# The low parts of the expert weights: from VectorE and GpSimd to VectorE alone, one operation per half chunk

## The reference

```python
def moe(x, w_router, b_router, w_gate_up, b_gate_up, w_down, b_down):
    logits = (x @ w_router) + b_router
    top_v, top_e = lax.top_k(logits, TOP_K)          # 4 of 32 experts for each row
    gates = jax.nn.softmax(top_v, axis=-1)
    ...
    def expert_block(args):
        xb, e = args
        h = xb @ w_gate_up[e] + b_gate_up[e]         # 1024 -> 2048
        gate = jnp.minimum(h[:, 0::2], SWIGLU_LIMIT)
        up = jnp.clip(h[:, 1::2], -SWIGLU_LIMIT, SWIGLU_LIMIT)
        glu = gate * jax.nn.sigmoid(gate * SWIGLU_ALPHA)
        return ((up + 1.0) * glu) @ w_down[e] + b_down[e]
    ...
    return jnp.sum(picked * gates[..., None], axis=1)
```

## Time and profile before

| | |
|---|---|
| times of three runs | 1637.43, 1633.67, 1636.84 us; median 1636.84 us |
| the profiled execution, from its first to its last instruction | 1633.7 us (no time of its own is given beside this span) |
| TensorE busy | 1552.0 us (95%) |
| VectorE busy | 1343.2 us (82%) |
| ScalarE busy | 937.3 us (57%) |
| GpSimd busy | 648.7 us (40%) |
| mean granted TensorE clock | 0.965 of full speed |

### The profile page before, as it was taken

The page is one execution under the profiler, slowest core; times in us unless marked ns, Lnnn a source line. Parts: engine busy times, 40 slices in busy tenths (PEclk is TensorE's granted clock), DMA queues, the critical chain, the costliest instruction groups (busy, mean ns, idle before and its releaser), DMA issues.

```text
span 1633.7 us, 19999 instructions
## 1 busy us (share of the span) xinstructions
PE 1552.0 (95%) x7028; PEld 1092.7 (67%) x7028; DVE 1343.2 (82%) x1571; ACT 937.3 (57%) x863; POOL 648.7 (40%) x229
## 2 busy tenths in 40 slices
PE   6999799959999999999999999999999999999992
PEld 4877585437676777776777777677777677767762
DVE  3034304469999999999999999999999999999995
ACT  2023411137666666666666666666666666666663
POOL 1011300024554444544445544555445544444443
PEclk9999859969999999999999999999999999999996
DMA  9300307138999999999999999999999999999974
GB/s 353 138 5 0 130 23 298 55 128 324 343 342 349 336 340 343 349 340 348 344 346 345 334 338 344 339 337 348 341 330 346 345 346 334 348 337 344 342 292 135
DMA packets 52241, 468.06 MB, mean 287 GB/s; under 512 B 9370, under 2 KB 13420, under 8 KB 27156
## 3 DMA queue, kind: packets, MB, share of 16 engines
q1 hardware_dynamic: 40676, 441.39, 71.2%
q0 software_dynamic: 9488, 22.99, 6.9%
q10 hardware_dynamic: 2032, 3.12, 0.6%
HBM read 451.15 MB, written 22.46 MB: 290 GB/s over the span
## 4 chain that ended last, share of the span: by engine, by line
PE 79%; DVE 4%; DMA 1%; issue 1%; ACT 0%; POOL 0%; DVEq 0%; ACTq 0%; POOLq 0%
PE psum L1497 23%; PE psum L1499 21%; PE psum L1498 21%; PE psum L1444 4%; PE psum L1511 3%; DVE low L1130 2%; PE psum L1467 2%; PE psum L1486 1%; PE psum L1477 1%; PE psum L1524 1%; PE psum L1427 0%; DMA y_tbl<-area,idx_i 0%; DVE ring L1187 0%; PE psum L1420 0%; ACT high L682 0%
## 5 line engine op out<-in xcount | busy, mean ns | idle before, releaser
L1130 DVE TENSOR_TENSOR low<-raw,high 128x1024 fp32r<-128x1024 f32 x645 | 953.3, 1532 | 24.9 <-ACT high L682 24.9
L682 ACT CAST high<-raw 128x2048 fp32r<-128x2048 f32 x387 | 732.6, 1909 | 179.7 <-PE psum L1499 168.5
L457 POOL TENSOR_TENSOR low<-raw,high 128x1024 fp32r<-128x1024 f32 x129 | 468.7, 3633 | 643.3 <-ACT high L682 630.1
L1497 PE MATMUL psum<-high,area_r 128*104 128x512 f32 x1536 | 621.9, 405 | 0.8 <-DVE area_r L1123 0.3
L1499 PE MATMUL psum<-low,area_r 128*104 128x512 f32 x1536 | 604.3, 393 | 0.0
L1498 PE MATMUL psum<-high,area_r 128*104 128x512 f32 x1536 | 604.1, 393 | 0.0
L1497 PEld LDWEIGHTS psum<-high,area_r 128*104 128x104 f32 x1536 | 257.9, 168 | 132.9 <-issue 45.9
L1499 PEld LDWEIGHTS psum<-low,area_r 128*104 128x104 f32 x1536 | 258.1, 168 | 96.3
L1498 PEld LDWEIGHTS psum<-high,area_r 128*104 128x104 f32 x1536 | 258.8, 168 | 83.4
L696 ACT ACTIVATE area<-area 104x512 f32<-104x512 f32 x64 | 40.5, 633 | 166.4 <-DVE area L1138 166.4
L1233 PE MATMUL psum<-ring 128*128 128x272 f32 x416 | 96.6, 393 | 0.0
(11 more groups left out here) (199 smaller groups left out, 1020.6 us busy)
## 6 DMA issues: line engine op xcount, KB each, us to landing
raw<-in_w_gate_up SPq DMA_DIRECT2D x130, 2048.0 KB, 10.3
raw<-in_w_down SPq DMA_DIRECT2D x64, 2048.0 KB, 8.2
ring<-in_w_in SPq DMA_DIRECT2D x1, 4096.0 KB, 37.0
area<-in_w_out SPq DMA_DIRECT2D x1, 4096.0 KB, 34.4
ring<-in_w_in SPq DMA_DIRECT2D x1, 3072.0 KB, 22.8
area<-in_x_prompt SPq DMA_DIRECT2D x4, 512.0 KB, 8.3
ring<-in_w_mem_kv SPq DMA_DIRECT2D x1, 2048.0 KB, 14.6
ring<-in_mem_kT SPq DMA_DIRECT2D x1, 2048.0 KB, 9.3
```

Source lines behind the costliest of these rows:

```text
L457: nc.gpsimd.tensor_tensor(low_w(t, 1, 2), raw_w(t, 1, 2), high_w(t, 1, 2), ALU.subtract).then_inc(sem("w_low_pool"), 1)
L682: nc.scalar.copy(high_w(t), raw_w(t)).then_inc(sem("w_high"), 1)
L1130: last = v.tensor_tensor(low_w(t, part, 2), raw_w(t, part, 2), high_w(t, part, 2), ALU.subtract)
L1497: mm(bank, high, wh, start=False, stop=False)
```

## The change

All twelve low parts of an expert come from VectorE, each in one operation of 2048 columns. GpSimd's `low_part` goes, and with it the semaphore `w_low_pool` and TensorE's wait on it.

```diff
-POOL_T = (2, 5, 8, 11)
...
-            def low_part(n, t):
-
-                pool.wait_ge(sem("w_high"), n * HALVES + (t + 1))
-                nc.gpsimd.tensor_tensor(low_w(t, 1, 2), raw_w(t, 1, 2), high_w(t, 1, 2), ALU.subtract).then_inc(sem("w_low_pool"), 1)
...
             def expert(n, k):
                 if not isinstance(n, int) or n > 0:
                     scatter(n, k)
-                low_part(n, 5)
                 gather(n + 1, k + 1)
-                low_part(n, 8)
-                low_part(n, 11)
-                low_part(n + 1, 2)
 
             gather(0, 0)
-            low_part(0, 2)
...
             def low_part(n, t):
 
-                parts = 1 if t in POOL_T else 2
                 dv.wait_ge(sem("w_high"), n * HALVES + (t + 1))
-                for part in range(parts):
-                    last = v.tensor_tensor(low_w(t, part, 2), raw_w(t, part, 2), high_w(t, part, 2), ALU.subtract)
-                last.then_inc(sem("w_low"), 1)
+                v.tensor_tensor(low_w(t), raw_w(t), high_w(t), ALU.subtract).then_inc(sem("w_low"), 1)
...
             def split_done(n, t):
 
                 pe.wait_ge(sem("w_low"), n * HALVES + (t + 1))
-                if t in POOL_T:
-                    pe.wait_ge(sem("w_low_pool"), n * len(POOL_T) + (POOL_T.index(t) + 1))
```

## The result

The changed kernel takes 1646.39 us (median of 4 runs, 1643.84 to 1648.30), against 1636.91 us before (4 runs): 9.5 us more, ratio 1.0065, 95% interval 1.005 to 1.008. The profiled execution spans 1646.5 us; its time was 1648.30, so 1.8 us lie outside the span.

A forecast was written before the change was run, and what follows sets the result against it. TensorE was taken to bound the kernel; 10.6 us of new wait less 1.3, 1.2 and 0.3 gave +7.8 us, profiled execution 1641.5 and median 1644.6. Range 1641 to 1650, or 1633 to 1650 with no new wait.

The forecast's parts named there:

- TensorE sets the pace: In the expert loop TensorE's matmuls bound the time, 38.855 us an expert; relieving VectorE by itself is worth nothing.
- The load itself: VectorE's work for each expert in the loop: 37.7 us before, 33.4 after, under TensorE's 38.855.
- The price of the long operation: A VectorE low part of 2048 columns lasts 2.285 us and takes 2.20 us of the queue.
- The freed memory: With GpSimd's part gone, VectorE's low parts run undisturbed: all within 2.26 to 2.35 us, none of 3 us or more.
- The new wait: TensorE waits for the second `act_low` ahead of half chunk 10: 0.33 us for each expert, 10.6 us in all.
- the handover from `act_low` to TensorE: Ahead of half chunk 10, TensorE's matmul starts 0.06 us after `act_low` ends, taken from one earlier case.
- The start gives back 1.3 us: Start of the loop: three VectorE operations take 6.60 us ahead of `x_low` where five took 7.92, so 1.3 us gained.
- The end gives back 1.2 us: End of the loop: without GpSimd's unneeded low part, the last scatter starts 0.19 us behind `yrow`, 1.2 us earlier.
- The median: Whole kernel: the profiled 1633.7 us was put 3.1 under the median of 1636.84; the median would go to 1644.6.
- The rivals: No new wait, 0.25; low parts keep their mean, 0.02; the freed engine is worth something, 0.05; a larger wait, 0.05.
- The case of no new wait: Rival: `act_low` is in time ahead of half chunk 10, leaving only the 2.8 us given back: 1634.0 us; chance 0.25.
- a slightly quicker TensorE: Rival: TensorE gains 0.1 us an expert with no new wait, 1630.8 us; 0.05 together with VectorE setting the pace.

The follow-up runs named there:

- twelve_ahead: The changed kernel with the low part of the next expert's half chunk 0 also ahead of the second `act_low`: 1744.2 us, 1.067 of the kernel before.
- only_eleven_pool: The changed kernel with the second 1024 columns of half chunk 11 given back to GpSimd: 1627.4 us, 0.994 of the kernel before.
- act_low_first: The changed kernel with the second `act_low` moved between the low parts of half chunks 10 and 11: 1627.1 us, 0.994 of the kernel before.
- eleven_to_dve: The kernel before with half chunk 11 alone taken from GpSimd, made by VectorE in two operations of 1024 columns: 1700.6 us, 1.038.

## Why the prediction was right, point by point

- **TensorE sets the pace, and VectorE's load doesn't.** Right: VectorE's busy share went from 194 to 180 us in 200, and the time rose. `twelve_ahead` shows it most plainly. The load itself was put too low, 33.4 us for each expert; measured are 179.77 / 200 x 39.29 = 35.3. The rest beside the low parts was taken as 7.0 from durations that count every overlap twice (20 x 1.535 = 30.7); the busy time in the earlier trace rows, 853.0 / 576 x 20 = 29.6, leaves 8.1. And the twelve long operations are busy for 871.8 / 387 x 12 = 27.0 us, not 26.4. With 4 us of slack left this cost nothing.
- **The price of the long operation: 2.285 us, of which 2.20 lie in the queue.** Measured 2285 ns in the median, and 821.74 to 826.15 for two, 2.205 each. The Trainium skill's formula (page "VectorE: DVE Perf Modes", section on the TRN2 errata) gives 2.29 us; the trace agrees within 0.01.
- **The freed memory.** Right: no operation over 2.295 us. In none of the six kernels without a low part on GpSimd does one of 2048 columns take over 2.30 us, or one of 1024 over 1.23. The trace agrees with the Trainium skill's rule that an operation of VectorE with two inputs and one of GpSimd that reads the memory lock each other out (page "SBUF — State Buffer", section "Who interferes with whom"): 3443 ns at most before, 2295 after. `only_eleven_pool` shows the other side: GpSimd's part takes 5.15 to 5.17 us each time, and none of VectorE's low parts is held up.
- **The new wait, 0.33 us for each expert, 10.6 us.** The place, the engines and the chain are right: swiglu at 0.43 us (measured 0.42), 2.73 us to the low parts (2.73), 4.40 for these (4.41). The size was 0.43 us and 13.8 us. The term that was mis-sized is the handover from `act_low` to TensorE: "the matmul started at 433.19, 0.06 later", where it is 0.13 us in the median of every kernel that waits there. That row lies in expert 1, ahead of the loop, where the handover is 0.06 us in each kernel; 28 of the 32 experts lie inside it. With it the same expert gives 0.40 us, as measured in the two shown (8.27 against 7.87); over all experts the old stretch is 7.83. And one step was misread: "Before, it started at 821.61, right behind the transposes". It started 0.13 us behind the end of `act_low`, 820.90 + 0.58 = 821.48, so it waited already. This wait of 0.21 us in each expert had no entry of its own, since the eight transposes are shown as lasting until 821.58. It cancels out of the difference of the two kernels: the change made a wait of 0.65 us out of one of 0.21. But it made the room for gain larger than I thought.
- **The start gives back 1.3 us.** Measured 1.2.
- **The end gives back 1.2 us.** Measured 1.2, but not in the way foretold: the scatter starts 0.96 us behind `yrow` instead of 0.19, as GpSimd now comes to it from idle (0.96 us is also the median in `act_low_first`), and it takes 1.61 us instead of 2.39 and lands 0.75 us sooner. That the sum of the two is again 1.2 is luck: in `act_low_first`, with the same queue on GpSimd, the last scatter takes 2.50 us and the end gives back 0.3.
- **The median.** I took the 1633.7 us of the profiled span for the time of that run. Its time was about 1635.5, with the 1.8 us that lie outside each span. This has no bearing on the difference.
- **The rivals.** None of them came. The case of no new wait, 1634 us, is what `act_low_first` was meant to show; it took 1627.1 because the old wait went too. That is also the gain that I had called "a slightly quicker TensorE": the possible gain was twice what I allowed for it, and it had a cause.

## What to carry to other kernels

As long as an engine with a queue in order has slack, work taken over from a helper is paid where it stands in the queue, and not by the engine's load; look at the chain that ended last to see that it still has, for in `eleven_to_dve` it had none and the price was 64 us. Look for the operation behind it that another engine waits for, here `act_low`, and put that one first: this turned 9.5 us of loss into 9.3 us of gain. And a chain without wait entries is no proof of slack: compare the handover, 0.13 us here from the end of one to the start of the other, with that of a case in which the wait is certain.

## What the runs showed of the hardware that I had not expected

- With 24 operations of 1024 columns for each expert in its loop of four, VectorE stood for 3.7 to 4.9 us at six of the seven turns, and the queue for instructions carried 50 transfers; with 21 or fewer it carried 19 to 21, and VectorE did not stand. Two kernels show it, at about 30 us each.
- TensorE's granted clock was 1.00 with a wait of 0.4 us in each expert, and fell for some microseconds to the lower level (products 0.43 us apart) behind waits of 2.1 and 2.6 us. In `twelve_ahead` not every expert with such a wait lost clock.
- The time that GpSimd takes to issue the scatter differs widely from kernel to kernel: in the median 2.39 us before, 1.65 in the changed kernel, 2.48 in `act_low_first`, whose queue on GpSimd is the same, and 6.60 in `eleven_to_dve`. The gather took 1.87, 2.37, 2.37 and 1.90. An empty queue is thus not what makes the scatter shorter; what does isn't shown.
